# Segment sums of the SSD block from turned running sums, 24 rows at a time in four row groups of the array

## The reference, cut to what matters

```
acum  = cumsum(dt * a_neg)                                   # over the 128 tokens of a chunk
seg   = acum[i] - acum[j]                                    # kept where j <= i, else -inf
decay = exp(seg)
cb    = C B^T                                                # 128 x 128, one for all 8 heads of a group
y_diag = (cb * decay) @ (dt * x)
states = B^T @ (x * dt * exp(acum[last] - acum))
h      = h * exp(acum[last]) + states                        # scan over the chunks
y_off  = (C h) * exp(acum)
y      = y_diag + y_off  (forward)  + the same backward  + D * x
```

## Time and profile before

| | |
|---|---|
| median of 3 runs | 2591.39 us (2589.88 to 2591.42) |
| the profiled execution | 2587.12 us |
| its span, first to last instruction | 2585.2 us |
| PE busy | 2236.9 us (87%) |
| DVE busy | 1090.4 us (42%) |
| ACT busy | 491.0 us (19%) |
| POOL busy | 379.7 us (15%) |
| mean granted TensorE clock | 0.922 |

### The profile page before, as it was taken

The page is one execution under the profiler, slowest core; times in us unless marked ns, Lnnn a source line. Parts: engine busy times, 40 slices in busy tenths (PEclk is TensorE's granted clock), DMA queues, the critical chain, the costliest instruction groups (busy, mean ns, idle before and its releaser), DMA issues. The chain is left out here.

```text
span 2585.2 us, 27166 instructions
## 1 busy us (share of the span) xinstructions
PE 2236.9 (87%) x9986; PEld 1389.0 (54%) x9986; DVE 1090.4 (42%) x1966; ACT 491.0 (19%) x1163; POOL 379.7 (15%) x373
## 2 busy tenths in 40 slices
PE   4789889799897889898988989879999978599986
PEld 2454554455543757576675757655555544443432
DVE  3564563664753354544535454420000018422224
ACT  0120221211211323233232323320000000011111
POOL 0041150141221020110102011000000000121112
PEclk9989989899898999898999989889999988599998
DMA  7010211101001110101011010149523063599983
GB/s 271 9 49 16 60 30 41 49 8 41 33 9 47 33 33 6 34 4 32 4 33 36 2 34 4 25 135 303 162 73 122 26 256 122 179 354 407 406 356 126
DMA packets 172782, 256.74 MB, mean 99 GB/s; under 512 B 14535, under 2 KB 141704, under 8 KB 158384
## 3 DMA queue, kind: packets, MB, share of 16 engines
q1 hardware_dynamic: 146136, 216.59, 24.0%
q10 hardware_dynamic: 18488, 23.54, 3.0%
q0 software_dynamic: 8096, 15.75, 1.7%
HBM read 229.33 MB, written 39.10 MB: 104 GB/s over the span
## 5 line engine op out<-in xcount | busy, mean ns | idle before, releaser
L649 PE MATMUL bank<-hT,shared 128*128 128x512 f32 x512 | 253.0, 629 | 13.4 <-DMA negm<-in_levels_dram 8.6
L1139 PE MATMUL bank<-hT,shared 128*128 128x512 f32 x384 | 175.4, 611 | 2.9 <-ACT spadded L1278 1.6
L2017 PE MATMUL bank<-ring,xgT 128*64 128x512 f32 (+1 forms) x416 | 148.7, 623 | 14.2 <-DMA ring<-in_w_exp_up_dram 10.4
L995 DVE TENSOR_TENSOR conv<-bank,negm 128x512 f32<-128x512 f32 x144 | 82.3, 599 | 184.4 <-PE bank L662 184.4
L649 PEld LDWEIGHTS bank<-hT,shared 128*128 128x128 f32 x512 | 94.6, 200 | 96.9 <-issue 88.1
L1219 PE MATMUL bank<-shared,hT 128*128 128x512 f32 x320 | 139.9, 592 | 0.0
L1599 DVE SCALAR_TENSOR_TENSOR prod<-gth,bank 128x512 f32<-128x512 f32 x16 | 11.0, 688 | 272.7 <-PE bank L1569 272.7
L662 PE MATMUL bank<-D_,MT 128*128 128x128 f32 x960 | 125.4, 279 | 0.0
L1139 PEld LDWEIGHTS bank<-hT,shared 128*128 128x128 f32 x384 | 73.9, 197 | 89.7 <-issue 85.9
L670 PE MATMUL bank<-DT,conv 128*128 128x128 f32 x960 | 121.6, 275 | 0.0
L1201 PEld LDWEIGHTS bank<-xT,M 128*128 128x128 f32 x640 | 88.4, 218 | 54.6 <-issue 41.2
(11 more groups left out here) (409 smaller groups left out, 3615.8 us busy)
## 6 DMA issues: line engine op xcount, KB each, us to landing
shared<-in_w_in_dram SPq DMA_DIRECT2D x58, 512.0 KB, 6.5
ring<-in_w_exp_gate_dram SPq DMA_DIRECT2D x26, 1024.0 KB, 12.5
ring<-in_w_exp_up_dram SPq DMA_DIRECT2D x26, 1024.0 KB, 19.5
ring<-in_w_exp_down_dram SPq DMA_DIRECT2D x26, 1024.0 KB, 14.7
aw<-in_w_ada_dram SPq DMA_DIRECT2D x8, 2048.0 KB, 9.9
yd<-mzero ACTq DMA_DIRECT2D x1, 16128.0 KB, 95.2
aw<-in_w_ada_dram SPq DMA_DIRECT2D x8, 1024.0 KB, 21.5
shared<-in_w_in_dram SPq DMA_DIRECT2D x4, 2048.0 KB, 7.9
```

What stands on the lines that cost most here:

```text
L649: last = pe.matmul(bank[a][:, :], w4[:, n, k, :], hT[:, k, SEQ:T], start=(k == 0), stop=(k == KD - 1), skip_group_check=True)
L995: TT(out=X[:, u0:u0 + n, :], in0=bank[XB[g]][:, 0:n * P].rearrange("p (u n) -> p u n", n=P), in1=m, op=ALU.mult).then_inc(s["g_Xkept"], 1)
L1139: pe.matmul(bank[a][:, :], wn(n)[:, k, :], hT[:, k, SEQ:T], start=(k == 0), stop=(k == KD - 1))
L2017: last = pe.matmul(bank[2 + slot][at, :], xgT[:, slot, k, at], wgu[w][:, k, :, :], start=(k == 0), stop=(k == KD - 1))
```

## The change

It replaces the way in which the segment sums are made, and what follows from that:

- **Running sums on PE.** DVE copies the 8 heads of `cur[:, 0]` into `wide` (20 blocks of 32 columns; 24 of the columns are constants, put there once before the loop). After `proj(2)` PE multiplies each block by C_LE or C_GE: 20 matmuls of 128 columns with 32 columns of weights, whose results lie at partitions 0, 32, 64 and 96 of banks 2 and 3. These are running sums with the token on the free axis.
- **Their copies on ACT.** Behind `raw(3)` ACT makes `fromT` (4 row groups, 8 rows each) and `uptoT` (4 heads, all rows) from them, with a scale and a bias of each partition: 16 activations, 8 of 512 columns and 8 of 128. `proj(4)` now waits for them (`s_cumkept`), since it writes the same banks.
- **The segment sums.** `seg(t)` makes both directions and all 8 heads of a tile in 4 matmuls of 512 columns and 24 rows, in row groups 0, 32, 64 and 96, each into a bank of its own. It is issued once a tile and waits until both exps of the tile before are taken. The product itself carries the mask, as a large negative number above the diagonal in blocks of 8 columns; what is left above it inside a block is caught by a minimum with 1 and by `cbm`.
- **`dec` goes.** ACT writes the exp into `M`, which has 4 slots, and DVE multiplies it in place: `min(M, 1) * cbm` in one instruction.
- **POOL** makes no `am`: it runs the five `skip` at once when the turned x is kept, then `xe`.
- **`keep_turn(3)` and `(4)`** on ACT stand behind the exps of u = 0 and 1 instead of behind that of u = 0.
- SP issues two more transfers of constants at the start of the stage; `zs` and `zth` use the slots of `M`.

```diff
+        edge = S("edge", [P, 2, 24])
+        wide = S("wide", [P, 4 * NT, 32])
+        fromT = S("fromT", [P, NT, P])
+        uptoT = S("uptoT", [P, NT, 4, P])
-        am = S("am", [P, 2, HG, P])
-        dec = S("sdec", [P, 2, HG, P])
-        M = S("M", [P, 2, HG, P])
+        M = S("M", [P, 4, HG, P])
...
             @block.sync
+                sp.dma_start(edge[:, :, :], small[:, S_EDGE:S_BEYOND].rearrange("p (d n) -> p d n", d=2)).then_inc(s["s_edge"], 16)
+                sp.dma_start(fromT[:, :, :], small[:, S_BEYOND:S_BEYOND + P].unsqueeze(1).broadcast_to([P, NT, P])).then_inc(s["s_beyond"], 16)
...
             @block.tensor
+                        if n == 4:
+                            pe.wait_ge(s["s_cumkept"], g + 1)
                         proj(n).then_inc(s["s_proj"], 1)
+                        if n == 2:
+                            pe.wait_ge(s["s_wide"], 1)
+                            pe.wait_ge(s["s_cur"], g + 1)
+                            for t in range(NT):
+                                for q in range(4):
+                                    last = pe.matmul(bank[2 + t // 4][32 * q:32 * q + 32, t % 4 * P:t % 4 * P + P], wide[:, 4 * t + q, :], C((C_LE, C_GE)[q // 2]),
+                                                     start=True, stop=True)
+                            last.then_inc(s["s_cum"], 1)
...
-                    def seg(u):
-                        pe.wait_ge(s["s_am"], 10 * g + u + 1)
-                        if u >= 2:
-                            pe.wait_ge(s["s_dec"], 10 * g + u - 1)
-                        for half_ in range(2):
-                            last = pe.matmul(bank[2 * (u % 2) + half_][:, :], C((C_GT, C_LT)[u % 2]),
-                                             am[:, u % 2, 4 * half_:4 * half_ + 4, :].rearrange("p h n -> p (h n)"), start=True, stop=True)
+                    def seg(t):
+
+                        if t == 0:
+                            pe.wait_ge(s["s_cumkept"], g + 1)
+                        else:
+                            pe.wait_ge(s["s_dec"], 10 * g + 2 * t)
+                        for q in range(4):
+                            rows = slice(32 * q, 32 * q + 24)
+                            last = pe.matmul(bank[q][:, :], fromT[rows, t, :], uptoT[rows, t, :, :].rearrange("p h n -> p (h n)"), start=True, stop=True)
                         last.then_inc(s["s_seg"], 1)
...
                     cbs(0)
                     seg(0)
                     turn(4, 3)
+                    cbs(1)
                     seg(1)
                     turn(5, 4)
                     for u in range(2 * NT):
                         t, d = u // 2, u % 2
-                        if 0 < u < 2 * NT - 1:
-                            if (u + 1) % 2 == 0:
-                                cbs((u + 1) // 2)
-                            seg(u + 1)
+                        if d == 0 and 0 < t < NT - 1:
+                            cbs(t + 1)
+                            seg(t + 1)
...
             @block.scalar
+                        if n == 3:
+                            act.wait_ge(s["s_cum"], g + 1)
+                            act.wait_ge(s["s_beyond"], 16)
+                            for q in range(4):
+                                rows = slice(32 * q, 32 * q + 8)
+                                scale, bias = cols[rows, S_FROM:S_FROM + 1], cols[rows, S_FROM + 1:S_FROM + 2]
+                                act.activation(fromT[rows, 0:4, :], bank[2][rows, :].rearrange("p (t n) -> p t n", n=P), ACT.Identity, bias=bias, scale=scale)
+                                act.activation(fromT[rows, 4, :], bank[3][rows, 0:P], ACT.Identity, bias=bias, scale=scale)
+                            for h in range(4):
+                                scale, bias = (cols[:, S_OWN + at + h:S_OWN + at + h + 1] for at in (0, 4))
+                                act.activation(uptoT[:, 0:4, h, :], bank[2][:, :].rearrange("p (t n) -> p t n", n=P), ACT.Identity, bias=bias, scale=scale)
+                                last = act.activation(uptoT[:, 4, h, :], bank[3][:, 0:P], ACT.Identity, bias=bias, scale=scale)
+                            last.then_inc(s["s_cumkept"], 1)
...
-                        if u == 1:
+                        if u == 2:
                             keep_turn(3)
                             keep_turn(4)
-                        act.wait_ge(s["s_seg"], 10 * g + u + 1)
-                        if u >= 2:
-                            act.wait_ge(s["s_M"], 10 * g + u - 1)
+                        act.wait_ge(s["s_seg"], 5 * g + u // 2 + 1)
+                        if u >= 4:
+                            act.wait_ge(s["s_y"], 10 * g + u - 3)
...
             @block.gpsimd
-                    for u in range(2 * NT):
-                        t, d = u // 2, u % 2
-                        if u >= 2:
-                            pool.wait_ge(s["s_seg"], 10 * g + u - 1)
-                        TT(out=am[:, d, :, :], in0=C((C_LE, C_GE)[d]).unsqueeze(1).broadcast_to([P, HG, P]),
-                           in1=cur[:, 0, t, d, :].unsqueeze(2).broadcast_to([P, HG, P]), op=ALU.mult).then_inc(s["s_am"], 1)
...
+                    pool.wait_ge(s["s_turnkept"], 5 * g + 5)
+                    for t in range(NT):
+                        skip(pool, s, TT, g, t, ysum, xt, dg, hv)
...
             @block.vector
+                dve.wait_ge(s["s_edge"], 16)
+                for t in range(NT):
+                    for d in range(2):
+                        ins = dve.tensor_copy(wide[:, 4 * t + 2 * d:4 * t + 2 * d + 2, 8:32], edge[:, d:d + 1, :].broadcast_to([P, 2, 24]))
...
-                    dve.engine_nop().then_inc(s["s_cur"], 1)
+                    heads = cur[:, 0, :, :, :].rearrange("p t d h -> p (t d h)").rearrange("p (u a) -> p u a", a=4)
+                    dve.tensor_copy(wide[:, :, 0:8].rearrange("p u (r a) -> p u r a", a=4), heads.unsqueeze(2).broadcast_to([P, 4 * NT, 2, 4])).then_inc(s["s_cur"], 1)
...
-                        TT(out=M[:, d, :, :], in0=dec[:, d, :, :], in1=cbm[:, t % 2, d:d + 1, :].broadcast_to([P, HG, P]), op=ALU.mult).then_inc(s["s_M"], 1)
+                        STT(out=M[:, u % 4, :, :], in0=M[:, u % 4, :, :], scalar=1.0, in1=cbm[:, t % 2, d:d + 1, :].broadcast_to([P, HG, P]),
+                            op0=ALU.min, op1=ALU.mult).then_inc(s["s_M"], 1)
```

More of the change, by code:

```diff
@@ L83 @@
 NSTEP = T // SLOT - 1
-S_ROW = S_STEP + NSTEP
+S_OWN = S_STEP + NSTEP
+S_FROM = S_OWN + 8
+S_ROW = S_FROM + 2
 S_PLACE = S_ROW + NP
 NCOL = S_ROW
+S_EDGE = S_PLACE + P
+S_BEYOND = S_EDGE + 2 * 24
+FAR = 1e4
 def small_constants():
@@ L91, in small_constants @@
     key = np.where(np.arange(NX) < NFIX, 1e5 - 1e3 * np.arange(NX), -np.arange(NX) / 64.0)
-    end = np.concatenate([np.arange(NMORE), key, SLOT * (1 + np.arange(NSTEP)), P * (1 + np.arange(NP)), np.arange(P)])
+    end = np.concatenate([np.arange(NMORE), key, SLOT * (1 + np.arange(NSTEP))])
+    last = np.concatenate([P * (1 + np.arange(NP)), np.arange(P)])
+    p, r, h = np.arange(P)[:, None], np.arange(P)[:, None] % 32, np.arange(4)[None, :]
+    own = np.concatenate([(r < 4) & (r == h), (r >= 4) & (r < 8) & (r - 4 == h), (r < 0) | (r >= 4), r < 4], 1).astype(np.float32)
+    own[:, 0:4] -= FAR * ((r >= 8) & (r < 24))
+    own[:, 8] *= -1
+    b = np.arange(24)[None, :]
+    edge = np.concatenate([1.0 * (p == 8 * b) - (p == 8 * b + 8), 1.0 * (p == 8 * b + 7) - (p == 8 * b - 1)], 1) * (np.tile(b, 2) < 16)
+    block = np.arange(P)[None, :] // 8
+    beyond = np.where(p < 64, block > r - 8, block < r - 8) * ((r >= 8) & (r < 24))
     tok = np.arange(P)[:, None] + P * np.arange(NT)[None, :]
-    return np.concatenate([np.broadcast_to(row, (P, row.size)), tok, np.broadcast_to(end, (P, end.size))], 1).astype(np.float32)
+    return np.concatenate([np.broadcast_to(row, (P, row.size)), tok, np.broadcast_to(end, (P, end.size)), own,
+                           np.broadcast_to(last, (P, last.size)), edge, beyond], 1).astype(np.float32)
 def positions():
@@ L201, in build @@
                 yT = sb("yT", [P, SH * SP_ // P, T], F32, bulk)
-                stage(ssd, bank, cst, C, hT, ST, cwT, vecT, half, shared, first_in, yT, w_in, ssd_d, state_ssd, new_ssd)
+                stage(ssd, bank, cst, C, cols, small, hT, ST, cwT, vecT, half, shared, first_in, yT, w_in, ssd_d, state_ssd, new_ssd)
                 oT = sb("oT", [P, KD, T], F32, bulk)
@@ L1034, in _, with ssd @@
                     assert st.n == DVE_STEPS, st.n
-def ssd(nc, sb, sem, bank, cst, C, hT, ST, cwT, vecT, half, shared, first_in, yT, w_in, ssd_d, state_ssd, new_ssd):
+def ssd(nc, sb, sem, bank, cst, C, cols, small, hT, ST, cwT, vecT, half, shared, first_in, yT, w_in, ssd_d, state_ssd, new_ssd):
     own = ExitStack()
@@ L1200, in body @@
                         for h in range(HG):
-                            last = pe.matmul(bank[6 + t % 2][:, h * SP_:(h + 1) * SP_], M[:, u % 2, h, :], dtx[:, u % 2, h * SP_:(h + 1) * SP_],
```

(12 more changed lines are left out.)

16 lines of the change are left out of this document (4 added, 12 removed).

## The result

| | before | after |
|---|---|---|
| median of 4 runs, us | 2591.26 (2589.88 to 2591.42) | 2639.09 (2634.71 to 2642.13) |
| span of the profiled execution, us | 2585.2 | 2638.1 |
| mean granted TensorE clock | 0.922 | 0.888 |

The ratio after to before is 1.0184 (95% interval 1.0167 to 1.0202): the change costs 48 us. The forecast was 2582 us with a range up to 2628; rival 1 gave 2640. The two profiled executions lie 52.8 us apart (2587.12 and 2639.96), since before's is 4.1 us under its median.

What follows compares the result with a forecast made beforehand. PE was taken to bound the middle tiles, with DVE close behind. Terms: 42.7 (running sums and copies) + 0.5 (way to first product) - 59 (products) + 7 (late clock) = -9 us, median 2582; range 2568 to 2628.

Steps and rivals of the forecast that it cites:

- rival 1: Products: the clock does not rise and they stay at half clock, 42.1 us a group, +48, 2640 us; chance 0.17.
- The products: Ten products of each group: 27.8 us instead of 40.8, with the states -14.8 a group, -59 for four groups.
- the allowance of 7: Products: +7 us for one group of four in which the clock rises one or two tiles later.
- Running sums: On PE: 40 instructions, about 1.2 us in the first group; in the others within the 3.69 us PE waits anyway.
- The copies: On ACT: 16 activations, 8.2 us, for which proj(4) waits; it starts 9.9 us later in the first group, +10.1 in others.
- cold stretch: First group, behind the idle ahead of proj(4): the clock drops, costing 2.5 us more.
- the way to the first product: From the projection to the first product: +0.5 us for all four groups, at most 3 either way.
- Row groups: Segment sums overlap as column groups do: 0.86 us a tile plus 0.1 for changing the array's layout.
- Rival 2: Segment sums: the row groups do not overlap, 3.43 us a tile, +33, 2624 us; chance 0.10.
- M in place: On DVE: the in-place instruction with a minimum priced as before, M at 1.2 everywhere past the first tile.
- the two new transfers of constants: Beside proj(0) and proj(1), priced at nothing with DVE's ten small copies; if not covered, about 2 us once.

Runs made afterwards that it cites:

- run 3: The changed kernel with every matmul of the sums issued four times (16 for each tile instead of 4): 2627.97 us, one run.
- run 4: run 1 plus two full-height filler matmuls ahead of each later C B^T (tiles 2 to 4), results overwritten: 2588.62 us, ratio 0.9998.
- run 2: The changed kernel with the same fillers as run 1, but of 24 rows in one row group: 2658.5 us, one run.
- run 1: The changed kernel with extra full-height matmuls, 4 behind seg(0) and 5 behind turn(5), results overwritten: 2634.71 us, ratio 1.0174.
- run 5: The kernel before with fillers, four behind the first segment sums and six behind the turn of channel tile 5: 2568.41 us, ratio 0.9923.
- the last versions: The changed kernel with exchanged banks, divided copies and fillers, two or one ahead of each later C B^T: 2551.07 us and 2542.68 us.

## Why the prediction was wrong

**The step that failed** is in "The products": "If it rises behind the sums of tile 2: 7.1 + 2.2, then 8 x 1.78 + 2 x 1.3, ...: 27.8 us instead of 40.8". The forecast took it that the 2.2 us of C B^T and row-group sums behind product 1 would raise the clock as 3.3 us of full-height sums had done in before. It did not rise in any of the four groups. The products took 42.45 us and the states 3.73, so the term was +6.6 us for four groups instead of -59. With the allowance of 7 that is 58.6 us of the 61.8 by which the profiled execution missed (-9 forecast, +52.8 measured; the medians moved by +48).

**Rival 1 is what happened.** It gave 10 x 3.55 + 3 x 2.2 = 42.1 us a group and 2640 in all; measured 42.45 and 2639.1. The products it had right; that the totals agree within 1 us is partly luck, since the profiled executions moved by 52.8 and not by its 48. It had a chance of 0.17, and its ground was in the earlier trace rows: the products alone had never raised the clock, and the segment matmuls between them shrank from 3.4 us a u to 1.7 a tile. Against it stood only that the sums are dense work. Run 3, which changes only the number of the sums' matmuls, shows that after has too little of them; run 4 shows that the same products run at full clock with full-height work among them. The Trainium skill ("TensorE: Matmul & The Clock Gate", Part 1) says that sustained work releases the clock. Runs 3 and 4 agree (0.82 and 1.00 in the first group's products against 0.50); run 2's 8.90 us of 24 rows and the 42.45 us of unbroken narrow products in after did not raise it, which that rule of the Trainium skill does not cover.

**What was priced right.**
- Running sums: 1.2 us forecast; 40 instructions in 1.30 with the tail.
- The copies: 8.2 us forecast, 8.7 measured. From `proj(2)` to `proj(4)` the first group took 10.5 us more (9.9 forecast), and its cold stretch cost 3.15 where 2.5 stood. In the other groups +10.1 was forecast and 10.3 came; DVE's four taps take 3.67 us there, as forecast. Sum of these terms with the way to the first product: 43.2 forecast, 41.3 + 3.8 = 45.1 measured.
- Row groups: 0.86 and 0.1 us a tile were forecast. In run 4 a tile's sums take 1.07 from start to the next start. In run 3 the 32 instructions ahead of the products take 3.72 at full clock, so 0.116 each against 0.46 (3.70 / 8) for run 1's full-height ones: four at a time. Rival 2 is out. The Trainium skill gives 3.07 times for this ("TensorE: Matmul & The Clock Gate", Part 3); here it was 4, and the measurement decides.
- With the clock up, the products: 27.8 us forecast with two of them cold; the first group of run 4 less its fillers gives 29.36 - 5.3 = 24.1 with none cold, and run 3 less its extra sums 27.2 with two cold, both estimates that leave out waits for M.
- M in place: 1.22 us. Beside POOL it is 2.06, for the first four of the ten, where the forecast had it in the first tile only.

**What was missed.** The stage starts 1.0 us late. SP issues the two new transfers of constants ahead of what releases PE's first projection; I had put them at nothing, beside `proj(0)` and `proj(1)`. PE's wait there (us, times, longest), before and after; it is 1.4 in run 5 as well and 2.4 in every run of the changed kernel:

```profile
PE bank L1139 <- SPq L1128: 1.4, 1, 1.4
PE bank L1157 <- SPq L1146: 2.4, 1, 2.4
```

And the allowance of 7 us was for a clock that is late in one group in four: I treated as a scatter of groups what is the same in all four.

**Not settled.** Whether two sets of sums would have done, between after's one and run 3's four; whether the fall of the clock in run 1 is due to the wait for M or to the narrow products around it; why one row group and four differ (runs 2 and 3); and why the clock dips in other groups from one execution of the last versions to the next.

## What to carry to other kernels

Before booking PE work that a change takes away as time gained, look at what it did for the clock. If it was the dense part of a stretch whose other matmuls are narrow or wait, the rest may run at half speed with PE shown as fully busy, as here (42.45 us of 42.45 at 0.50), and the granted clock of the stretch says so. The test is cheap: matmuls that compute nothing, put where PE waits. A bank that slow readers hold costs their time if the next matmul writes it (8.9 us of wait for 8.7 us of copies in the first group); once that is mended the reader's own order can be the next bound, and here only 26 to 28 of the 48 us of waiting came back.

## What the runs showed that I had not expected

- Matmuls of 24 rows in one row group, 3.80 and 8.90 us of them, neither held nor raised the clock, where full-height ones of the same count did both (runs 1 and 2). The clock rose within the 6.72 us of sums in four row groups side by side (run 3).
- Fillers of no use to the computation made the kernel before 0.77% faster (0.61 to 0.94%).
- Four row groups of fp32 matmuls overlapped fully (0.116 us each against 0.46), and changing from full height to 24 rows and back cost an estimated 0.1 to 0.2 us a tile (1.07 from start to next start, where 8 x 0.116 is 0.93).
